# A split-weight Strassen feed-forward block: the down weights in half pieces, and another order of the seven products in a unit

## The reference, cut to what matters

```python
def swiglu(h, w_gu, w_down):
    gu = h @ w_gu                      # [512, 1024] @ [1024, 5632]
    g, u = jnp.split(gu, 2, axis=-1)
    return (jax.nn.silu(g) * u) @ w_down   # [512, 2816] @ [2816, 1024]

x = x + swiglu(rms_norm_2(x, ffn_norm[l]), ffn_w_gu[l], ffn_w_down[l])
```

## Time and profile before

| | |
|---|---|
| median of 3 executions | 1955.8 us (1955.07 to 1957.76) |
| the profiled execution's own time | 1952.36 us |
| its span from first to last instruction | 1950.6 us |
| TensorE (PE) busy | 1883.7 us, 97% of the span |
| VectorE (DVE) busy | 1450.2 us, 74% |
| ScalarE (ACT) busy | 1210.0 us, 62% |
| GpSimd (POOL) busy | 272.4 us, 14% |
| mean granted TensorE clock | 0.996 of full speed |

### The profile page before, as it was taken

How to read it: one execution, slowest core, us unless ns; L and a number is a source line. 1 busy time by engine, 2 the same in 40 slices (tenths; PEclk the granted TensorE clock), 3 DMA queues, 4 the chain that set the end, 5 groups by cost and what they waited for, 6 DMA issues and landing times.

```text
span 1950.6 us, 26707 instructions
## 1 busy us (share of the span) xinstructions
PE 1883.7 (97%) x10258; PEld 1582.1 (81%) x10258; DVE 1450.2 (74%) x1826; ACT 1210.0 (62%) x1786; POOL 272.4 (14%) x339
## 2 busy tenths in 40 slices
PE   5999999999999999999999999999999999999997
PEld 4668768888888888858889899897777779989896
DVE  6677699998999999872557866869444557776868
ACT  4443268888888888844346655657555546655565
POOL 3111210122211101020011011111011111011011
PEclk9999999999999999999999999999999999999999
DMA  8465579999999999962326686775321225777773
GB/s 302 161 216 195 180 260 372 366 378 376 377 377 365 362 369 369 338 220 74 108 66 157 157 199 169 164 187 146 106 65 53 78 76 110 176 191 190 178 169 115
DMA packets 221004, 415.50 MB, mean 213 GB/s; under 512 B 14762, under 2 KB 95543, under 8 KB 219850
## 3 DMA queue, kind: packets, MB, share of 16 engines
q1 hardware_dynamic: 181296, 343.73, 49.5%
q0 software_dynamic: 31008, 59.38, 15.8%
q10 hardware_dynamic: 8570, 10.64, 1.6%
HBM read 381.30 MB, written 24.65 MB: 208 GB/s over the span
## 4 chain that ended last, share of the span: by engine, by line
PE 71%; DVE 11%; DMA 8%; ACT 5%; issue 4%; POOL 1%; ACTq 0%; POOLq 0%; DVEq 0%
PE ps L448 68%; DVE wlo L393 3%; DMA raw<-in_ffn_w_gu 3%; DMA raw<-sums 3%; ACT whi L363 2%; PE ps L2411 1%; DMA raw<-in_ffn_w_down 1%; DVE sums L286 1%; DVE X L3145 1%; ACT raw L255 1%; PE ps L2438 1%; DMA VR<-in_b_subln 1%; DVE ATl L3127 1%; DVE XN L3157 0%; PE ps L3428 0%
## 5 line engine op out<-in xcount | busy, mean ns | idle before, releaser
L393 DVE TENSOR_TENSOR wlo<-raw,whi 128x1024 fp32r<-128x1024 f32 (+1 forms) x638 | 749.2, 1212 | 136.0 <-ACT whi L363 131.6
L363 ACT ACTIVATE whi<-raw 128x1024 fp32r<-128x1024 f32 (+1 forms) x638 | 639.4, 1046 | 232.5 <-PE ps L448 122.3
L448 PE MATMUL ps<-whi,ATh 128*128 128x512 f32 x308 | 121.0, 393 | 6.3 <-DVE X L3145 6.3
L448 PE MATMUL ps<-wlo,ATh 128*128 128x512 f32 x308 | 120.1, 390 | 0.0
L448 PE MATMUL ps<-whi,ATl 128*128 128x512 f32 x308 | 120.0, 390 | 0.0
L448 PE MATMUL ps<-whi,XT0h 128*128 128x512 f32 x256 | 102.9, 402 | 1.7 <-DVE XT0l L2494 1.7
L448 PE MATMUL ps<-whi,XT1h 128*128 128x512 f32 x256 | 102.8, 402 | 1.5 <-DVE XT1l L2494 1.5
L448 PE MATMUL ps<-hT3h,whi 128*128 128x256 f32 (+1 forms) x352 | 103.6, 294 | 0.6 <-DVE hT3l L445 0.6
L448 PE MATMUL ps<-hT5h,whi 128*128 128x256 f32 (+1 forms) x352 | 103.2, 293 | 0.6 <-DVE hT5l L445 0.6
L448 PE MATMUL ps<-hT3l,whi 128*128 128x256 f32 (+1 forms) x352 | 103.4, 294 | 0.0
L448 PE MATMUL ps<-hT3h,wlo 128*128 128x256 f32 (+1 forms) x352 | 103.4, 294 | 0.0
(11 more groups left out here) (529 smaller groups left out, 4894.0 us busy)
## 6 DMA issues: line engine op xcount, KB each, us to landing
raw<-in_w_expert_gate SPq DMA_DIRECT2D x64, 1024.0 KB, 7.3
raw<-in_w_expert_up SPq DMA_DIRECT2D x64, 1024.0 KB, 8.1
raw<-in_w_expert_down SPq DMA_DIRECT2D x64, 1024.0 KB, 6.9
raw<-in_ffn_w_gu SPq DMA_DIRECT2D x44, 1024.0 KB, 7.5
raw<-in_ffn_w_down SPq DMA_DIRECT2D x16, 1024.0 KB, 9.6
raw<-in_ada_w SPq DMA_DIRECT2D x24, 512.0 KB, 4.8
raw<-in_ffn_w_gu POOLq DMA_DIRECT2D x20, 512.0 KB, 5.9
raw<-sums POOLq DMA_DIRECT2D x20, 512.0 KB, 5.6
```

The lines of the kernel that those rows point to most:

```text
L363: e.activation(hi[:, c], x, ACT.Copy).then_inc(self.S("w_hi"), 1)
L393: e.tensor_tensor(lo[:, c], raws[h], hi[:, c].bitcast(F32), ALU.subtract).then_inc(self.S("w_lo"), 1)
L448: return e.matmul(o, l, r, start=start, stop=stop, skip_group_check=True)
```

## The change

Three things are moved, with no arithmetic more or less.

1. The down weights no longer go through three whole buffers of 2048 columns but, like the up weights, through the six half buffers, as two pieces a product (`split` twice in `quad`, 2 chunks and `a - 2` chunks).
2. A unit of the up part runs its products in a new order, `UP_ORDER = (1, 2, 5, 6, 3, 7, 4)`. SiLU of the early tokens moves on ACT from product 4 to product 5, and `gate` part 1 on DVE from behind product 2 to behind product 3.
3. In the last unit before a down part, the last two chunks of the row sum for product 5 and its split, and the row sum for product 6 are made behind products 7 and 4, and no longer after the unit. In the down part `add` of product 5 comes ahead of a row sum. Between a down part and the next unit the negations and splits on ACT are put in another order.

```diff
+UP_ORDER = (1, 2, 5, 6, 3, 7, 4)
...
         for p in order:
             (i, at), t = of[p]
-            made[p] = self.split(name, i, a, 512 if at is None else 256,
-                                 after=None if t is None else (self.S(f"sum{t}"), (q + 1) * (1 if t == 2 else 16)), at=at)
+            after = None if t is None else (self.S(f"sum{t}"), (q + 1) * (1 if t == 2 else 16))
+            if at is None:
+                self.split(name, i, 2, 512, after=after, at=0)
+                made[p] = self.split(name, i, a - 2, 512, after=after, at=1024)
+            else:
+                made[p] = self.split(name, i, a, 256, after=after, at=at * a * 256)
...
-                W.places = [0, 1, 2]
...
@@ ffn_plan @@
-                    for p in ORDER:
+                    for p in UP_ORDER:
                         name = f"up{l}.{n}.{p}"
                         R.plan(name, 1, V_ if p in (3, 7, 2) else A_, on=collections.deque([v if p in (5, 3) else y if p == 2 else z]))
...
@@ ffn_act @@
                     copy(n, p, LATE[1][:, :, :])
+                    e.wait_ge(*R.done(f"up{l}.{n}.2"))
+                    e.activation(FA[:, at, EARLY_T], FA[:, at, EARLY_T], ACT.Silu).then_inc(S("silu"), 1)
...
-                    for m, p in enumerate(ORDER):
+                    for m, p in enumerate(UP_ORDER):
                         j = up_pieces(l, n)[m]
-                        W.high(e, j + W.depth(j))
-                        if m == 0:
+                        after_down = f == 0 and m == 0
+                        W.high(e, j + 4 if after_down else j + W.depth(j))
+                        if m == (1 if f == 0 else 0):
                             W.negate_over(e, q + 1)
...
@@ ffn_vec @@
+                        if m == 5 and f == fn - 2:
+                            cs = slice(a - 2, a)
+                            e.wait_ge(*gated(l, n, 1))
+                            e.tensor_tensor(a21[:, cs, :], a21[:, cs, :], a22[:, cs, :], ALU.add).then_inc(S("s_sum"), 1)
+                        if m == 6 and f == fn - 2:
+                            low(gi, a, 1, a - 2)
+                            e.wait_ge(S("left_lo"), splits(l, gi, 1))
+                            e.tensor_tensor(a21, a21, a11, ALU.subtract).then_inc(S("s_sum"), 1)
                         if p == 3:
                             gather(n, p, LATE[0][:, :, :])
+                            gate(n, 1)
                         if p == 7:
                             gather(n, p, LATE[1][:, :, :])
...
                 W.low(e, js[3] + 1)
                 low(gi, a, 3)
+                for tb in range(2):
+                    add(f0, 5, tb)
                 e.wait_ge(S("s_sum"), summed(l, gi, 4))
                 e.tensor_tensor(a21, a22, a21, ALU.subtract).then_inc(S("s_sum"), 1)
```

More of the change, by code:

```diff
@@ L218, in halves @@
         i, a, b = self.w[j]
-        if self.at[j] is None:
+        at = self.at[j]
+        if at is None:
             n = a * b // 2
[L221 to L225, removed]
+            return [self.raw[self.raw_of[i][0]][:, h * n:(h + 1) * n] for h in range(2)]
+        x = self.total(self.quad_of[j], False)[0] if i is None else self.raw[self.raw_of[i][0]]
+        return [x[:, at:at + a * b]]
     def wide(self, q):
@@ L845, in ffn_plan @@
                     R.plan(name, 2, V_, on=collections.deque(v if p in (5, 3) else y if p == 2 else z))
-                    W.ends[W.index[f"fd{l}"][nd]] = R.full(name, 1)
-                    nd += 1
+                    for j in W.index[f"fd{l}"][nd:nd + 2]:
+                        W.ends[j] = R.full(name, 1)
+                    nd += 2
                 R.turn.extend(v + y + z)
@@ L2977, in product @@
                 k = 7 * (gi % 3) + m
-                j = W.index[f"fd{l}"][k]
-                w, x = W.parts(j), [operand(i, k, a) for i in range(2)]
+                js = W.index[f"fd{l}"][2 * k:2 * k + 2]
+                ws, x = [W.parts(j) for j in js], [operand(i, k, a) for i in range(2)]
                 for tb in range(2):
@@ L2982, in product @@
                     for kc in range(a):
[L2983 to L2987, removed]
+                        if tb == 0 and kc % 2 == 0:
+                            e.wait_ge(*W.lowered(js[kc // 2]))
+                        if tb == 0 and (kc == 0 or m == 1 and kc == a - 2):
+                            e.wait_ge(S("left_lo"), splits(l, gi, m, 0 if m == 1 and kc == 0 else 1))
+                        i = mm3(e, b[:, :], [y[:, kc, tb * P:(tb + 1) * P] for y in x], [y[:, kc % 2, :] for y in ws[kc // 2]],
                                 kc == 0 and p in (1, 5, 2), kc == a - 1)
@@ L3050, in ffn_act @@
                 e.activation(FA[:, k, :], R.bank(f"fg{l}", k)[:, :], ACT.Silu).then_inc(*R.free(f"fg{l}", k))
+            W.high(e, first + 3)
             for i in range(4):
@@ L3054, in ffn_act @@
                     W.negate_total(e, q)
-                    W.high(e, first + 3)
+                    W.high(e, first + 4)
             n = 1
@@ L3076, in ffn_act @@
                             high(gi, f0, a, 1, 0, a - 2)
+                        if m == 6 and f == fn - 2:
+                            e.wait_ge(S("s_sum"), summed(l, gi, 2))
+                            high(gi, f0, a, 1, a - 2)
                         if f == 0 and m == 0:
@@ L3081, in ffn_act @@
                     q += 1
[L3082 to L3085, removed]
                 for m in range(2, 7):
+                    if m == 6 and f0 + fn < 22:
+                        W.negate_over(e, q + 1)
                     W.high(e, js[m] + 1)
@@ L3091, in ffn_act @@
                     if m == 2:
+                        W.negate_first(e, q)
                         W.negate_total(e, q)
@@ L3094, in ffn_act @@
                 if f0 + fn < 22:
-                    W.negate_over(e, q)
                     W.high(e, js[6] + 3)
                     W.negate_first(e, q)
+                    W.high(e, js[6] + 4)
                     W.negate_total(e, q)
@@ L3180, in ffn_vec @@
             sum_low(0)
-            W.low(e, first + 2)
+            W.low(e, first + 3)
             sum_low(1)
@@ L3186, in ffn_vec @@
             sum_low(2)
-            W.low(e, first + 3)
+            W.low(e, first + 4)
             for k in range(2):
@@ L3225, in ffn_vec @@
                             gather(n, p, FA[:, chunks(n), EARLY_T])
-                        if p == 4:
-                            gate(n, 1)
                     n += 1
                     q += 1
-                cs = slice(a - 2, a)
-                e.wait_ge(*gated(l, n - 1, 1))
-                e.tensor_tensor(a21[:, cs, :], a21[:, cs, :], a22[:, cs, :], ALU.add).then_inc(S("s_sum"), 1)
+                gate(n - 1, 2)
                 W.low(e, js[1] + 1)
[L3234 to L3237, removed]
                 W.low(e, js[2] + 1)
@@ L3249, in ffn_vec @@
                 for m in range(4, 7):
-                    for tb in range(2):
-                        add(f0, ORDER[m - 3], tb)
+                    if m > 4:
+                        for tb in range(2):
+                            add(f0, ORDER[m - 3], tb)
                     W.low(e, js[m] + 1)
@@ L3261, in ffn_vec @@
                         if m < 6:
-                            W.low(e, js[6] + (3 if m == 4 else 5))
+                            W.low(e, js[6] + m)
                 else:
```

18 lines of the change are left out of this document (9 added, 9 removed).

## The result

The changed kernel takes **2025.37 us** (2022.22 to 2027.31, 4 executions) against 1956.78 us (1955.07 to 1960.62, 4 executions) for the kernel before: ratio **1.036** [1.0344, 1.0376]. It is slower, as forecast, but by 69 us and not by 26, and lies outside the range of 1964 to 1998.

What follows compares the result with a forecast made beforehand. The prediction took PE, busy 1883.7 of 1950.6 us, to bound the kernel, so only its idle time counted. 47.2 us lost less 20.4 gained gave +26.8, stated as 1982 us, range 1964 to 1998.

Steps and rivals of the forecast that it cites:

- What bounds the kernel, and what was gained: Whole kernel: only PE's idle time counts; removed copy waits, add waits and slow clock stretches gain 20.4 us.
- copies and adds in question: PE's 5 waits for the copy of product 1 and 7 for a down-part `add`: 9.4 and 8.0 us gained.
- 1.03 us a unit: Product 4 waits for the gather of 7 on bank `z`: 1.03 us each in 14 units, 14.4 us.
- the price of the first units: Four first units after a down part: late `sum1` pushes the gather of 7 by about 0.4 us, 1.6 in all.
- Last units: Six last units of groups: DVE late for the gather of 7, 4.4 us in four, 2.3 in two; 22.2 together.
- counted DVE work: Last units: DVE work from gather of 3 to gather of 7, counted at 5.95 us against product 7's 2.88.
- Clock: Behind the six last-unit waits PE falls to 1.2 GHz, 1.5 us each: 9.0 us lost.
- Half pieces at nothing: Down weights split in half pieces: same bytes and operations, effect hidden behind ACT's waits for PE, 0 us.
- Last units no worse: Rival: DVE keeps up in last units and clock stays steady; +1.8 us, 1957.6 us, chance 0.08.
- the relief wins: Rival: bank `z` comes back sooner, at 0.69 us a unit; -6.6 us, 1949 us, chance 0.07.
- The clock oscillates: Rival: each of 14 short gather waits also brings a 1.2 GHz stretch; 21 us more, 2003 us, chance 0.07.

Runs made afterwards that it cites:

- Experiment 3: Changed kernel with negation first in units after a down part and, in last units, gather of product 7 ahead of the sums: 1966.52 us, ratio 1.0039.
- Experiment 6: Changed kernel, negation still late, with the two 1 MB loads in first units after a down part held until `sum1` lands: 2005.37 us, ratio 1.0225.
- experiment 1: Changed kernel with the negation for `sum1` again ahead of the copy of product 1 in first units after a down part: 1984.42 us, ratio 1.0135.
- experiment 2: Changed kernel with the gather of product 7 ahead of the two sums and row sum in last units of a group: 2004.98 us, ratio 1.0247.
- experiment 7: Changed kernel with order 1, 2, 6, 5, 7, 3, 4, early negation, and gate, row sum, gather and some splits moved: 1939.66 us, ratio 0.9893.
- experiment 4: Changed kernel with product 2 back between 7 and 4, SiLU, gate and row sums back, negation early: 1952.31 us, ratio 0.9968.

## Why the prediction was wrong in size

- **What bounds the kernel, and what was gained: right.** All copies and adds in question are gone, and with them both slow stretches of the earlier trace rows in the layers; 20.5 us for 20.4.
- **1.03 us a unit: right.** 0.94 and 0.10 for the first matmul in nine of ten. Experiment 3 shows it bare in fifteen of its twenty units.
- **The failed step is the price of the first units**, "`sum1` (5.9 us, rows 11) then lands some 13 us into the unit, and `sums`, a `wlo` and the rest push the gather of 7 by about 0.4: 1.6". The mechanism was named, its size was not worked out. Landing is at 22.5 us and the push 7.8 to 9.2. Two things were missed. The negation waits behind the split for `sum4`, whose DMA lands only 8.6 us into the unit, so the issue is at 11.0 and not near 7: the prediction names these splits, but I set no time against them. And 5.9 us was taken from a place where the DMA goes out ahead of the loads (2.5 us ahead in this unit of the kernel before), while here two loads go out at the same moment. That two like DMAs took 9.1 and 10.6 in the earlier trace rows had shown that such a duration is not fixed; I used that spread for the last units and not here. Experiment 6 measures the second part, experiment 1 the whole. With the first units like the rest the forecast would be 1982 less 1.6, and experiment 1 took 1984.4.
- **Last units: right**, 22.7 for 22.2, and experiment 2 shows the counted DVE work to be the cause: with 2.88 of the 5.95 us moved behind the gather, the first of them falls from 4.84 to 1.74.
- **Clock: right for the places foreseen**, 8.1 for 9.0, five of six; that it was right to this point is in part luck, since waits of this length do not always bring a fall, as the last section shows. Behind the four longest waits it cost 9.3 more, which belongs to the failed step.
- **Half pieces at nothing: right in time**, as a sum of shifts that I had not seen; this is luck in part.
- **The rivals.** "Last units no worse" and "the relief wins" fall with the counted waits. "The clock oscillates" falls too: fifteen waits of 0.78 us idle in experiment 3, none with a slow stretch behind it, and nine such waits here. Four windows of after, with the granted clock third from the end:

```profile
1095.40:1102.20 6.80, 4.03 (x19) 4.03 (x20) 4.63 (x6) 1.58 (x2) 0.00 (x0) 0.50 0.00 0
...
1163.70:1173.90 10.20, 4.78 (x22) 4.78 (x23) 7.63 (x8) 3.94 (x4) 1.74 (x2) 0.50 0.54 103
...
1354.80:1358.20 3.40, 3.40 (x19) 3.40 (x18) 1.43 (x2) 0.00 (x0) 0.00 (x0) 0.50 0.00 0
1980.00:1983.40 3.40, 3.40 (x27) 3.31 (x28) 1.65 (x2) 0.59 (x2) 0.00 (x0) 1.00 0.00 0
```

The three at 0.50 belong to the waits of 4.68, 9.95 and 2.24 us shown above; the first two begin while PE still stands. None in the layers of the changed kernel belongs to a wait under 2 us. The Trainium skill, "TensorE: Matmul & The Clock Gate", section "A second HAM failure mode: psum-queue depth-cycling", on which the rival drew, describes another kernel, which cycles through PSUM banks and idles briefly between groups of matmuls, and whose clock goes up and down. Here one bank is claimed with such a wait every 21 us, and the trace shows no such clock.

## What to carry to other kernels

When an instruction is moved on an in-order engine, work out the new issue time of every DMA that hangs on it, with a clock time for each wait that now stands ahead of it; a list of instructions shows the order and not the time. Price the transfer beside what will be moving at the new time, not by its duration when alone. And where accumulating products take turns on a bank, choose the order so that no two neighbours use the same one: the relief then came without a wait for the gather (experiment 7, against 1.03 us a unit in experiment 3).

## What the runs showed of the hardware

- An adding DMA of 512 KB on POOL's queue took 5.8 us with the loads held back, 5.8 issued 2.5 us ahead of two loads of 1 MB (kernel before), 8.4 behind two other adding DMAs and 11.5 issued together with two such loads, of which one took 5.9 and the other 11.2. Behind two loads that had gone out 2.8 us earlier, one took 9.4 (experiment 4).
- A wait of one length does not decide the clock. After two waits of 2.24 us idle, both in units with the same instructions, it was 0.50 behind the first (1354.8) and 1.00 behind the second (1980.0), as the windows above show. In the waits of about 10 us it read 0.50 before PE started again (from 1163.63, where PE's last matmul had begun at 1158.89 and the next came at 1169.12), and stayed there for 10.2 us, against 3.4 behind most of the shorter waits. In the layers of all nine traces no wait under 1.90 us idle was followed by a fall, and between 1.90 and 2.58 some were and some were not (2.50 was not, in experiment 2 at 1233.31). What decides it stays open.
